# Two fused transformer blocks on one core: embedding projected first, input chunks in paired products, norms in whole rows, last rows loaded one by one

## What is computed

```python
# first block
hn = rms_norm(h, g_mix_pre[i])
u = hn @ w_in[i]                       # xr, q, k, v, yg: 5 x 1024 columns
...
gate = jax.nn.sigmoid(rms_norm(h, g_ple_pre[i]) @ w_ple_gate[i])
ple = p[i] @ w_ple_proj[i]             # 256 x 256 @ 256 x 2048: "the embedding"
h = h + rms_norm(gate * ple, g_ple_post[i])
# second block
mix = token_mix(h, pos, w_in[l], ...)
x = layer_norm(DN_ALPHA * x + g1 * mix, ln1_g[l], ln1_b[l])
h = layer_norm(x) * (1.0 + sc2) + sh2
ffn = peer(h, w_pq[l], sub_key_1[l], sub_key_2[l], u_table[l], v_table[l])
x = layer_norm(DN_ALPHA * x + g2 * ffn, ln2_g[l], ln2_b[l])
```

## Time and profile before

| | us |
|---|---|
| median of 3 runs | 3263.34 (3259.12 to 3263.57) |
| profiled execution | 3258.77 |
| its span | 3257.2 |
| TensorE busy | 3144.6 (97%) |
| DVE / ACT / POOL busy | 2225.2 / 1421.4 / 733.6 |

### The profile page before, as it was taken

The page is one execution under the profiler, slowest core; times in us unless marked ns, Lnnn a source line. Parts: engine busy times, 40 slices in busy tenths (PEclk is TensorE's granted clock), DMA queues, the critical chain, the costliest instruction groups (busy, mean ns, idle before and its releaser), DMA issues.

```text
span 3257.2 us, 45091 instructions
## 1 busy us (share of the span) xinstructions
PE 3144.6 (97%) x17162; PEld 2699.4 (83%) x17162; DVE 2225.2 (68%) x2625; ACT 1421.4 (44%) x1438; POOL 733.6 (23%) x514
## 2 busy tenths in 40 slices
PE   8999899999999997999969999999999999999997
PEld 6989788888877876888759999888888788888885
DVE  6666888788778877456688996666665555555556
ACT  4556543343334455445543444433434344434342
POOL 1100000000000000000000888888883110000100
PEclk9999999999999998899989999999999999999998
DMA  7444677777779864584324777877866766666662
GB/s 258 168 176 173 233 254 279 277 275 279 279 275 338 306 237 173 202 333 153 143 103 169 227 213 224 258 251 252 259 212 230 268 238 243 238 243 238 243 237 106
DMA packets 195300, 754.34 MB, mean 232 GB/s; under 512 B 53826, under 2 KB 53858, under 8 KB 124786
## 3 DMA queue, kind: packets, MB, share of 16 engines
q1 hardware_dynamic: 129988, 664.86, 56.7%
q0 software_dynamic: 55984, 71.19, 7.8%
q10 hardware_dynamic: 9216, 16.78, 1.4%
HBM read 714.82 MB, written 37.93 MB: 231 GB/s over the span
## 4 chain that ended last, share of the span: by engine, by line
PE 64%; DVE 4%; DMA 2%; issue 1%; ACT 1%; POOL 0%; DVEq 0%; SPq 0%; ACTq 0%; POOLq 0%
PE bank L424 15%; PE bank L426 15%; PE bank L425 15%; PE bank L430 11%; PE bank L431 5%; DVE misc L2090 1%; DMA ring<-in_down 1%; DMA misc<-gelu_dram 0%; PE bank L510 0%; PE bank L881 0%; DVE raw_lo L1931 0%; PE bank L1096 0%; PE bank L1094 0%; PE bank L499 0%; DVE hid_parts L2220 0%
## 5 line engine op out<-in xcount | busy, mean ns | idle before, releaser
L430 PE MATMUL bank<-h_both,ffn_hi 128*128 128x512 f32 x2880 | 1007.7, 396 | 2.1 <-DVE raw_lo L2193 2.1
L2608 DVE TENSOR_TENSOR part_lo<-ring,ffn_hi 128x2048 fp32r<-128x2048 f32 x256 | 586.8, 2293 | 352.6 <-ACT ffn_hi L1826 351.6
L1826 ACT ACTIVATE ffn_hi<-ring 128x2048 fp32r<-128x2048 f32 x252 | 482.8, 1916 | 643.0 <-PE bank L426 327.7
L430 PEld LDWEIGHTS bank<-h_both,ffn_hi 128*128 128x128 f32 x2880 | 540.6, 188 | 141.7 <-issue 12.1
L2916 POOL DMA_INDIRECT weight_dram<-misc x256 | 580.6, 2268 | 87.9 <-issue 75.4
L431 PE MATMUL bank<-h_both,part_lo 128*128 128x256 f32 x1472 | 410.0, 279 | 0.0
L424 PE MATMUL bank<-ffn_hi,coef_hi 128*128 128x512 f32 x1024 | 399.1, 390 | 4.9 <-DVE coef_lo L2742 4.9
L426 PE MATMUL bank<-ffn_hi,coef_lo 128*128 128x512 f32 x1024 | 399.1, 390 | 0.0
L425 PE MATMUL bank<-part_lo,coef_hi 128*128 128x512 f32 x1024 | 399.0, 390 | 0.0
L1931 DVE TENSOR_TENSOR raw_lo<-ring,ffn_hi 128x2048 fp32r<-128x2048 f32 (+1 forms) x132 | 300.3, 2279 | 140.9 <-ACT ffn_hi L1369 140.1
L431 PE MATMUL bank<-h_both,raw_lo 128*128 128x256 f32 x1408 | 390.7, 278 | 0.0
(11 more groups left out here) (395 smaller groups left out, 5536.1 us busy)
## 6 DMA issues: line engine op xcount, KB each, us to landing
ring<-in_u_table SPq DMA_DIRECT2D x128, 1024.0 KB, 4.8
ring<-in_v_table SPq DMA_DIRECT2D x128, 1024.0 KB, 4.8
misc<-in_w_ada SPq DMA_DIRECT2D x192, 512.0 KB, 5.6
ring<-in_gateup SPq DMA_DIRECT2D x88, 1024.0 KB, 4.8
ring<-in_first SPq DMA_DIRECT2D x56, 1024.0 KB, 4.8
ring<-in_down SPq DMA_DIRECT2D x44, 1024.0 KB, 7.2
ring<-in_stream SPq DMA_DIRECT2D x40, 1024.0 KB, 5.0
ring<-in_wo_pq SPq DMA_DIRECT2D x32, 1024.0 KB, 4.8
```

The lines of the kernel that those rows point to most:

```text
L430: nc.tensor.matmul(out[:, 0:2 * S], hi, x_pair, start=start, stop=False)
L1826: a.activation(part_hi[j % PARTS], raw[j % RAW], ACT.Copy).then_inc(sem("hi_ready"), 1)
L2608: v.tensor_tensor(part_lo[j % PARTS], raw[j % RAW], part_hi[j % PARTS].bitcast(F32), ALU.subtract).then_inc(sem("lo_ready"), 1)
```

## The change

Five things are changed.

1. `pT` is loaded by ACT's queue at the very start; PE waits for it and for the first embedding weights alone. The second embedding weights are loaded ahead of chunk 0. Three panels run ahead of the transposes, the fourth after transposes 0 to 3. Four of the eight copies of the panels go to DVE (`ple_out_v`).
2. Chunk 0's products are interleaved with the transposes, piece by piece. Chunks 0 and 1 are split before the pieces on ACT, and chunk 0 and half of chunk 1 are lowered before them on DVE. Part of the softplus series moves to DVE's wait for x, the rest behind the first convolution. ACT loads its table for roots ahead of time, by a root of a constant.
3. The 24 chunks of xr, q and k use `paired_products`. DVE adds the halves (`x_sum`) ahead of each convolution, and ACT's 24 copies are gone.
4. The norm before the queries works on whole rows of 2048. Half 0's second statistics are made on ACT: a sum, a negated mean, and a sum of squares about it. The last norm subtracts and scales by the gain in one whole-row instruction while ACT takes the root, and then scales and shifts on DVE in halves; ACT's passes are gone.
5. The three last rows are loaded one at a time, after every eighth round of the pairs' loop.

```diff
@@ tensor
-            pe.wait_ge(sem("consts_in"), 16 * 3)
-            pe.wait_ge(sem("ones_set"), 1)
+            pe.wait_ge(sem("pT_in"), 16)
...
+            for c in range(3):
+                pproj_panel(c)
+            pe.wait_ge(sem("consts_in"), 16 * 2)
+            pe.wait_ge(sem("ones_set"), 1)
+            pe.wait_ge(sem("x_normed"), 1 + T)
+            for k in range(4):
+                x1_turn(k)
+            pproj_panel(3)
+            pe.wait_ge(sem("ple_copied"), 3)
+            wait_lo(pe, 0)
+            for k in range(KD):
+                ks = slice(k * P, (k + 1) * P)
+                pe.wait_ge(sem("x_lo_out"), TURN_AT["n1"] + k + 1)
+                if k + 4 < KD:
+                    x1_turn(k + 4)
+                m = paired_products(out_bank("xr", 0), ffn_hi[0][:, ks], raw_lo[0][:, ks], x1_hi[:, k, :],
+                                    x1_pair(k), k == 0, k == KD - 1)
...
-                stationary_chunk(pe, ("xr", "q", "k")[n // 8], n % 8, x1_hi, x1_lo)
+                stationary_chunk(pe, ("xr", "q", "k")[n // 8], n % 8, x1_hi, x1_lo, pair=x1_pair)
@@ scalar
+            a.dma_start(pT[:, :, :], io["pT"]).then_inc(sem("pT_in"), 16)
...
+            ple_out(0)
+            ple_out(1)
             root()
...
-            for o in range(4):
-                ple_out(o)
+            upper_in(0)
+            upper_in(1)
...
-                if k == 5:
-                    upper_in(0)
-                if k == 13:
-                    for o in (6, 7):
-                        ple_out(o)
-            upper_in(1)
+                if k == 3:
+                    ple_out(4)
+            ple_out(5)
             upper_in(2)
...
-                if 1 <= n < 25:
-                    copy_out(("xr", "q", "k")[(n - 1) // 8], (n - 1) % 8, places[n - 1], chunk=(n - 1) % 8, width=S)
...
+            a.wait_ge(sem("h2_first"), 1)
+            steps.mark(a.activation(nat[:, 0, :], resid[:, 0, :], ACT.Copy, accum_out=st[:, 28:29]))
+            steps.wait()
+            steps.mark(a.activation(st[:, 29:30], st[:, 28:29], ACT.Copy, scale=-1.0 / D))
+            root(1, 3, 1)
+            steps.wait()
+            a.activation(nat[:, 0, :], resid[:, 0, :], ACT.Square, bias=st[:, 29:30], accum_out=st[:, 31:32]).then_inc(
+                sem("h2_squares"), 1)
+            upper_in(SPLIT_PQ + 1)
             root(0, 2, 1)
-            root(1, 3, 1)
+            upper_in(SPLIT_PQ + 2)
             h2_half(0, 0, D)
@@ vector
+            def x_sum(m):
+                phase, j = ("xr", "q", "k")[m // 8], m % 8
+                wait_multiplied(v, phase, j)
+                v.tensor_reduce(places[m], halves(out_bank(phase, j)), AXX, ALU.add).then_inc(taken, 1)
...
+                if 1 <= n < 25:
+                    x_sum(n - 1)
                 if 1 <= n <= RB:
                     conv(n - 1)
...
-                scales2(t, None)
+                one_root(t, 1.0, EPS_LN, mv[:, t, 1:2], lambda: mark(v.scalar_tensor_tensor(
+                    out=result[:, t, :], in0=resid[:, t, :], scalar=mv[:, t, 0:1], in1=last_rows[1],
+                    op0=ALU.subtract, op1=ALU.mult)))
...
-                    v.wait_ge(sem("last_normed"), 2 * t + half + 1)
-                    link(v.tensor_tensor(result[:, t, cs], result[:, t, cs], last_rows[1][:, cs], ALU.mult))
-                    v.tensor_tensor(resid[:, t, cs], result[:, t, cs], last_rows[2][:, cs], ALU.add).then_inc(
+                    v.scalar_tensor_tensor(out=resid[:, t, cs], in0=result[:, t, cs], scalar=st[:, 16 + t:17 + t],
+                                           in1=last_rows[2][:, cs], op0=ALU.mult, op1=ALU.add).then_inc(
@@ gpsimd
-            for n, (name, m) in enumerate(((None, G2), ("ln2_g", 0), ("ln2_b", 0))):
-                row_in(last_rows[n], name, sem("rows_in"), mod_dram[m:m + 1, :] if name is None else None)
...
+            for n, (name, m) in enumerate(((None, G2), ("ln2_g", 0), ("ln2_b", 0), (None, None))):
+                rounds = NEB // PARTS // 4 if n < 3 else NEB // PARTS - 1 - done
...
+                if m is not None:
+                    row_in(last_rows[n], name, sem("rows_in"), mod_dram[m:m + 1, :] if name is None else None)
```

## The result

The changed kernel took 3235.77 us (median of 4 runs, 3234.01 to 3237.62) against 3261.23 for the kernel before beside it: ratio 0.9921, 95% interval 0.9909 to 0.9934, so 25.5 us less. The prediction was 3234. Its profiled execution took 3237.62, 21.2 us less than that of before, with a span of 3236.0. In what follows a wait of TensorE is counted from the start of the last product before it to the start of the next one; the idle time in brackets in the profile's lines is some 0.3 to 0.6 us less.

A forecast was written before the change was run, and what follows sets the result against it. TensorE, busy 97% of the span, was taken as the bound. 10.6 + 4.8 - 0.5 + 4.2 + 4.0 + 4.1 = 27.2 us gave 3231.6 (profiled execution) or 3236.1 (median); 3234 was taken, range 3226 to 3248.

The forecast's parts named there:

- The start: Embedding, transposes and chunk 0: chunk 0 done at 32.8 instead of 43.4 us, gain 10.6, bounds 4.7 and 11.6.
- half the gain lost to the low clock: Rival at the kernel's start: TensorE falls to the low clock, chunk 0 ends 5.9 us later, 3240; chance 0.12.
- The paired chunks: 23 chunks of xr, q and k: paired step 0.35 instead of 0.36 us, gain 4.8, bounds 2.3 and 5.3.
- The late load at the gates: Early xr chunks: chunk 4's slow load may stall TensorE once, 0.5 us lost, at best 0, at worst 5.
- The norm before the queries: Whole-row passes 1.8 and half 0's statistics on ACT 2.7, less 0.3: gain 4.2 us, bounds 3.0 and 4.6.
- The last rows: Third pair of values: its load no longer waits behind three 1 MB rows, stall gone, 4.0 us, 3.0 to 4.2.
- The last norm: Behind TensorE's last product: each half takes 5.4 instead of 7.45 us, together 4.1, range 3.4 to 4.1.
- DVE's line: Rival in the first chunks: sum, convolution and lowering queue behind late loads, TensorE waits up to 5 us, 3239; chance 0.10.
- the clock: Rival at the start: low clock granted while TensorE waits around 19 or 24 us, costing 5.9 us, 3240; chance 0.12.

The follow-up runs named there:

- r3: Changed kernel with all sixteen transposes back ahead of chunk 0's first product: 3237.43 us.
- r2: Changed kernel with the pairing undone, chunks 1 to 23 of xr, q and k back to three products a step: 3238.55 us.
- r9_same: Changed kernel unaltered, measured once more on another chip: 3235.29 us against 3262.97 for the kernel before.
- r8: Changed kernel with the sixteen short bias-row loads issued two at a time behind chunks 4 to 11: 3232.35 us.
- r6: Changed kernel with half 0's second statistics back on DVE, whole-row passes kept: 3238.58 us.
- r4: Changed kernel with the embedding's input loaded on POOL's queue again, fourth behind the constants: 3239.48 us.
- r5: Changed kernel with the three last rows loaded one behind the other ahead of the pairs' loop again: 3241.6 us.
- r11: Changed kernel with useless products in five TensorE waits and bias rows loaded two at a time: 3226.58 us, ratio 0.9886 to the kernel before.
- r7: Changed kernel with the last norm as before, ACT scaling in halves, DVE multiplying and adding: 3237.68 us.
- r10_filler: Changed kernel with useless products in two TensorE waits, 44 before the feed-forward part and 9 before its second chunk's low part: 3232.04 us.

## Why the prediction was right

*The start, 10.6.* 10.96 in the first trace. Step by step: panels from 6.97 (forecast 6 to 7), chunk 0 from 24.10 (24.0), 0.58 a step (0.57), done at 32.6 (32.8). Its rival, half the gain lost to the low clock, is what the order without interleaving runs into (r3), and not the order of the change.

*The paired chunks, 4.8.* Too much: 3.0 by r2, 3.4 in the first trace (a lead of 12.5, less 11.0 for the start, and 1.9 for the gates added), about 4 in r9_same, which has more of the fast pace. The term took the pitch of 0.346 for all 23 chunks. The text had the other value too, 5.66 a chunk, as its lower bound of 2.3, and had seen it in the first chunks of the feed-forward part. The mistake was to hold those for an exception; they are what a paired stream does in part of each execution (16 steps of 0.353 are 5.65).

*The late load at the gates, -0.5.* Too little: -1.9. The line was right (load, split, lowering, sum, convolution, gates), and r8 shows its cause. The term's mistake was the load's 11.8 us, taken from before and put down to the store and the short rows together. There the store had landed 0.9 us before the load was issued; now the load was issued 0.6 us behind the store and took 13.1. The bounds, 0 to -5, held it.

*The norm before the queries, 4.2.* 4.5 measured; 3.0 and 1.5 by r6, where the prediction had 2.7 less 0.3 and 1.8. But 1.6 to 2.7 us of it are given back by 1927 us. Behind the wait for the second chunk's low part, the same 1.86 us in both, the clock fell once more in the changed kernel (first fence) and not before it (second):

```profile
1696.00:1699.00 3.00, 1.42 (x7) 0.80 0.46 139
1699.00:1702.00 3.00, 3.00 (x19) 0.63 0.50 210
```

```profile
1708.00:1711.00 3.00, 1.29 (x7) 1.00 0.23 57
1711.00:1714.00 3.00, 3.00 (x26) 1.00 0.70 292
```

In r3, r4 and r5, whose clock stayed at 1.00 behind this wait, only 0.1 to 0.5 us are given back.

*The last rows, 4.0.* The mis-sized term: 5.7. The wait was read rightly, 4.0, and the load lands in time as forecast. What the list of waits does not hold is the time behind the wait, 1.7 us at the low clock in the trace of before. A window laid over it would have shown 0.50 there.

*The last norm, 4.1.* 4.3.

The sum of the measured steps, 11.0 - 1.9 + 3.4 + 4.5 + 5.7 + 4.3, is 27.0, against 27.2 forecast. That is partly luck: pairing and gates came 2.8 short and the rows 1.7 over. And none of it reckoned with the leak, 5.8 us in the first trace and 2.8 and 3.5 in the two others. In the first trace 3.1 us of it go before 531 us and 1.7 behind the norm before the queries. In each of the two the clock fell behind a short wait behind which it had stayed up in the kernel before, and the slow pace of the pair has a part in the first. The rest, 3.3 lost in the down part and some 2 regained up to 1657.9, is not the clock's: r11 loses 3.0 us in the down part at a clock of 1.00, and three executions of one program lose 3.3, 0.9 and 2.0. So the theory of the clock is shown for the feed-forward part's start, where filling the waits brought 3.3 to 3.7 us, and wrong for the down part.

The forecast of 3234 was helped by its start as well. Counted from the profiled execution of before the sum gives 3231.6, and the profiled execution took 3237.62, 6 us more. The 3234 lay halfway between that and the sum counted from a median, 3236.1. The medians fell by 25.5, 33.0 and 27.7; in the first comparison the median of before is 2.5 us above its profiled execution. Of the rivals none came true; two of them were at work in part, DVE's line and the clock.

What stays open: what decides whether the low clock follows a short wait (r7 and r9 differ in nothing before it), which of its two paces the paired stream takes up after an interruption, and why the down part loses 0.5 us in one execution and 4 in another.

## What to carry to other kernels

A wait on TensorE costs more than its length: price it with the granted clock of the stretch behind it, from the windows, and not from the list of waits. Where such a wait can't be removed, products without use in a free bank keep the clock up, and pay if TensorE is what the restart hangs on; look first whether another engine sets the pace there. What is started earlier at the front meets the traffic of the old schedule, so read which transfer is in flight where the new first load will be issued, and price a small transfer by its place in its queue.

## What was not expected of the hardware

The same wait of 2.64 us was followed by the low clock in most executions and not in others of the same code up to there, at 1.4 to 1.5 us each time. The paired stream (one product of 512 and one of 256 columns, with their weights) has two steady paces, about 0.347 and 0.353 us a step. It keeps one of them as long as nothing else is multiplied, and changes only where other products stand between: behind gates in the 24 chunks (as at 157 to 163 us, where in all eleven traces with pairing there the fast ones turned slow and the slow ones fast), and in the feed-forward part behind the two places where L896 multiplies (at 447 and 493 us in the first trace). There it is fast for good from about 460 us in the kernel before, from 496 in the changed one and from 446 in r10_filler. A load of 1 MB that usually takes 4.8 us took 9.5 with one store of 2 MB in flight, 11.8 with loads of short rows, and 13.1 with both.
